# A transformer block with a mixture of 16384 experts on one core: the matrix of gates added into DRAM entry by entry in place of one-hot matrix products, and deeper rings of loaded data

## The chip, the cores and the metric

The kernel runs on one core of one Trainium2 chip. The metric is the time of one execution in microseconds (us) on the device, given as the median of several runs. A core has five engines that work side by side: PE multiplies matrices, DVE does vector operations, ACT does activations and copies, POOL does general work and issues indirect DMAs, SP issues DMAs. They wait for each other through semaphores. Sixteen DMA engines carry what SP, ACT and POOL issue.

## What is computed

The program is a block with retention and sparse attention, a convolutional feed-forward part, then a second block with a gated recurrence and, last, the part that the change is in: PEER, a layer of 16384 experts of which each of the 512 tokens uses 8 x 16.

```python
def peer(h, w_query, sub_keys, expert_u, expert_v):
    ...
        q = (xb @ w_query).reshape(T, PEER_HEADS, 2, PEER_HALF)
        s = jnp.einsum('thpk,hpnk->thpn', q, sub_keys).astype(jnp.float32)
        top_s, top_i = lax.top_k(s, PEER_TOPK)
        cand_s = top_s[:, :, 0, :, None] + top_s[:, :, 1, None, :]
        cand_i = top_i[:, :, 0, :, None] * PEER_NKEYS + top_i[:, :, 1, None, :]
        best_s, best_pos = lax.top_k(cand_s.reshape(T, PEER_HEADS, PEER_TOPK * PEER_TOPK), PEER_TOPK)
        idx = jnp.take_along_axis(cand_i.reshape(T, PEER_HEADS, PEER_TOPK * PEER_TOPK), best_pos, axis=-1)
        gate = jax.nn.softmax(best_s, axis=-1)
        ...
        act = jax.nn.gelu(jnp.einsum('td,thkd->thk', xb, u).astype(jnp.float32), approximate=False)
        return jnp.einsum('thk,thkd->td', (gate * act).astype(xb.dtype), v)
```

## The kernel before

All matrices stream through a ring of four chunks of 512 KB. For each chunk SP loads RAW, ACT rounds it to WH (`split_high`, a "high"), DVE computes the rest WL (`split_low`, a "low"), and PE multiplies by three products (`mm3`, lines 272 to 274). A high waits until PE has used the chunk four before it. The order of the work on each engine is written out by hand, as numbers of chunks.

The last two stages belong to the experts. In the **u stage** (144 chunks `p`, of which 16 are the query matrix) PE computes the product of all 512 tokens with the 128 keys of every chunk, ACT applies gelu (`gelu`, L1101), and SP keeps the result in DRAM (`acts`). At the same time DVE finds for each tile `t` of 128 tokens the 16 best of each list (`pairs`), subtracts the largest (`shifted`), and turns places into the numbers n1 and n2 of the expert (`summed`, with a comparison prepared on POOL by `places_apart`, L795). `listed` ends it with the softmax weight.

For three of the four tiles (ND = 3) the gates must lie in DRAM as a matrix of experts by tokens. PE turns the three lists (L2184), DVE writes for 8 tokens at a time one-hot rows of n1 and of n2 times weight (`onehot_rows`, L1707 and L1710, from a difference that POOL makes at L807), PE multiplies them (`gates_of`, L2172, 48 groups n), ACT moves the products to a staging area (`store_gates`, L1123) and stores it six times (L1126). The fourth tile goes another way: POOL picks its rows of `peer_v` (L814, `pick_row`) and single activations (L822, `pick_acts`), and DVE sums them (L1739, `sum_row`).

In the **v stage** (128 chunks `v`) ACT loads gates and acts for four chunks at a time (`load_group`, L1129 and L1130, a ring of two groups), DVE multiplies them (`weights`, L1719), ACT takes the high part (L1135), DVE the low part WGL (L1723), and PE multiplies both with the chunk of `peer_v`. The first two groups are loaded by ACT in chunk p = QU - 6 = 138 of the u stage:

```python
                if p == QU - 6:
                    for r in range(2):
                        act.wait_ge(sem(f"gates_written{r}"), 16 * NU // 2)
                    ...
                    for j in range(2):
                        load_group(j)
```

`low_of_next(n)` does the next n lows; `lows[0]` counts them. L267 is the low, L261 the high.

Of the kernel before, what the change touches and what calls it, by code (L numbers as in the profile page):

```python
# [21 lines left out]
P = 128  # L22
# [23 lines left out]
NU = DW // 64  # L46
NG8 = 8 * NU
PICKS = PH * TOPK
SLOTS = 6
# [30 lines left out]
LOWS_LISTED = (47, 59, 71, 77)  # L80
LOWS_SHIFTED = (35, 47, 59, 71)


def before_gates(n):
    return 80 + 3 * n // 4

def constants():  # L90
# [27 lines left out]
    cols["token"] = (GT_TILE * P + i[:, None]).astype(f)  # L118
# [7 lines left out]
    for n, m in enumerate((64, 32, 16, 8, 4, 2, 1)):  # L126
# [7 lines left out]
              ("causal", P), ("cmp_ok", NT * 32), ("cmp_no", NT * 32), ("iota", P), ("four", 4), ("token", 1)]  # L134
# [12 lines left out]
def build(nc, d):  # L147
# [3 lines left out]
    with ExitStack() as ctx:  # L151
# [485 lines left out]
        LST = [A[:, 21504:21888], A[:, 21888:22272], XF[:, 0:384]]  # L637
        LST = [x.rearrange("p (l t) -> p l t", l=3) for x in LST]
        APART = XF[:, 2048:4096].rearrange("p (r i n) -> p r i n", r=2, i=8)
        zg, zs8 = misc(8), misc(8)  # L640

        HALF = 64
        STG = A[:, 0:16384].rearrange("p (r i t) -> p r i t", r=2, i=P)
        OHA = A[:, 16384:18432].rearrange("p (r n) -> p r n", r=16)
        OHB = A[:, 18432:20480].rearrange("p (r n) -> p r n", r=16)

        ACTED = [GATE[:, 0, 0:512], GATE[:, 0, 512:1024], ROW[:, 0:512], ROW[:, 512:1024]]
        G4 = A[:, 0:8 * DW].rearrange("p (r u i t) -> p r u i t", r=2, u=NU, i=4)
        AC = A[:, 8 * DW:16 * DW].rearrange("p (r i t) -> p r i t", r=2, i=4)
        WGHr = over("A", "WGH", 16 * DW, 4 * DW, F32R).rearrange("p (r t) -> p r t", r=4)  # L650
        WGLr = over("A", "WGL", 20 * DW, 4 * DW, F32R).rearrange("p (r t) -> p r t", r=4)
        WGH = WGHr.bitcast(F32)
        WF = A[:, 24 * DW:26 * DW].rearrange("p (r t) -> p r t", r=2)


        ROWS = A[:, 26 * DW:26 * DW + SLOTS * D].rearrange("p (r n) -> p r n", r=SLOTS)
        assert 26 * DW + SLOTS * D <= 16384
# [12 lines left out]
        acts_kept = nc.dram_tensor("acts", (P, P, S), F32, kind="Internal").ap()  # L670
        act_list = acts_kept.rearrange("e p (t o) -> (e p t) o", o=1)
# [75 lines left out]
        def _(pool):  # L747
# [35 lines left out]
            pool.dma_start(ROW[:, :], dr["nf_post"].partition_broadcast(P)).then_inc(sem("row_landed"), 16)  # L783
            pool.wait_ge(sem("rows_weighted"), 2 * NT)
# [5 lines left out]
            def places_apart(t, i):  # L790

                wait(pool, "eq_summed", 4 * t + i)
                p3 = PAB.rearrange("p s u -> p (s u)")[:, i * 64:i * 64 + 64].rearrange("p (h k) -> p h k", k=TOPK).unsqueeze(3)
                it = con("iota")[:, 0:TOPK].unsqueeze(1).unsqueeze(1)
                nc.gpsimd.tensor_tensor(EQ, p3.to_broadcast([P, PH // 2, TOPK, TOPK]),  # L795
                                        it.to_broadcast([P, PH // 2, TOPK, TOPK]), ALU.subtract).then_inc(sem("eq_ready"), 1)
# [5 lines left out]
            pool.wait_ge(sem("list_stored"), ND)  # L802
            pool.wait_ge(sem("picks_listed"), 1)
            for n in range(NG8):
                wait(pool, "onehot_ready", n - 1)
                nums = LST[n // 16][:, 1, 8 * (n % 16):8 * (n % 16) + 8].unsqueeze(2).to_broadcast([P, 8, P])
                nc.gpsimd.tensor_tensor(APART[:, n % 2], con("iota").unsqueeze(1).to_broadcast([P, 8, P]), nums,  # L807
                                        ALU.subtract).then_inc(sem("rows_apart"), 1)

# [16 lines left out]
            for r in range(2):  # L826
                pool.wait_ge(sem(f"gates_written{r}"), 16 * NU // 2)
# [16 lines left out]
        def _(act):  # L844
# [268 lines left out]
            gm = dr["gate_matrices"]  # L1113

            def store_gates(n):
                u = n // 8
                if n % 8 == 0:
                    wait(act, f"gates_written{u % 2}", 16 * (u // 2))
                for b in (2 * n, 2 * n + 1):
                    act.wait_ge(sem("gm_ready"), b + 1)  # L1120
                    at = 4 * (b % 16)
                    dst = STG[:, u % 2].rearrange("p i t -> p t i")[:, at:at + 4, :]
                    nc.scalar.activation(dst, PS[:, b % 4, :].rearrange("p (t n) -> p t n", t=4), ACT.Copy)                        .then_inc(sem("gm_stored"), 1)  # L1123
                if n % 8 == 7:
                    act.wait_ge(sem("gm_stored"), 16 * (u + 1))
                    act.dma_start(gm[u], STG[:, u % 2]).then_inc(sem(f"gates_written{u % 2}"), 16)  # L1126
# [10 lines left out]
            for p in range(24, QU):  # L1137
                high_of_next()
                gelu(u_of(p))
                for t in range(NT):  # L1140
                    if p == LOWS_SHIFTED[t] - 3:
                        act.wait_ge(sem("best_shifted"), t + 1)
                        nc.scalar.activation(BV[:, t % 2], BV[:, t % 2], ACT.Exp).then_inc(sem("best_exp"), 1)
                    if t < ND and p == LOWS_LISTED[t] - 2:
                        act.wait_ge(sem("list_turned"), t + 1)
                        nc.scalar.activation(LST[t], PS[:, 4, 0:3 * P].rearrange("p (l t) -> p l t", l=3), ACT.Copy)                            .then_inc(sem("list_stored"), 1)
                for n in range(NG8):
                    if before_gates(n) == p + 1:
                        store_gates(n)
                if p == QU - 6:  # L1150
                    for r in range(2):
                        act.wait_ge(sem(f"gates_written{r}"), 16 * NU // 2)
                    for r in range(4):
                        act.wait_ge(sem(f"acts_kept{r}"), 16 * 2)
                    for j in range(2):
# [33 lines left out]
        def _(dve):  # L1189
# [289 lines left out]
            for m in range(28):  # L1479
# [12 lines left out]
                if m == 6:  # L1492
                    dve.wait_ge(sem("hg_exps"), 1)
                    link(nc.vector.tensor_tensor_scan(flat(BB), flat(SC8), flat(HF), 0.0, ALU.mult, ALU.add))
# [146 lines left out]
            def summed(t, i):  # L1641

                dve.wait_ge(sem("eq_ready"), 4 * t + i + 1)
                for h in range(PH // 2):
                    num = TFf[:, i * 64 + 16 * h:i * 64 + 16 * h + TOPK].unsqueeze(1).to_broadcast([P, TOPK, TOPK])
                    last = nc.vector.scalar_tensor_tensor(EQ[:, h], EQ[:, h], 0.0, num, ALU.is_equal, ALU.mult)
                last.then_inc(sem("eq_numbers"), 1)
                dve.wait_ge(sem("eq_numbers"), 4 * t + i + 1)
                nc.vector.tensor_reduce(N12[:, t % 2].rearrange("p s u -> p (s u)")[:, i * 64:i * 64 + 64],
                                        EQ.rearrange("p h k a -> p (h k) a"), AX, ALU.add).then_inc(sem("eq_summed"), 1)  # L1650

            def listed(t):
                assert lows[0] == LOWS_LISTED[t]
                dve.wait_ge(sem("best_exp"), t + 1)
                dve.wait_ge(sem("eq_summed"), 4 * t + 4)
                link(nc.vector.tensor_reduce(zg, BV[:, t % 2], AX, ALU.add))
                link(nc.vector.reciprocal(zg, zg))
                if t < ND:
                    nc.vector.tensor_tensor(BV[:, t % 2], BV[:, t % 2], zg.unsqueeze(2).to_broadcast([P, PH, TOPK]),
                                            ALU.mult).then_inc(sem("list_ready"), 1)  # L1660
                else:
                    n1, n2 = N12[:, t % 2, 0], N12[:, t % 2, 1]
                    nc.vector.tensor_tensor(GW.rearrange("p (h k) -> p h k", h=PH), BV[:, t % 2],
                                            zg.unsqueeze(2).to_broadcast([P, PH, TOPK]), ALU.mult)
                    link(nc.vector.scalar_tensor_tensor(EXPERT, n2, float(P), n1, ALU.mult, ALU.add))
# [17 lines left out]
            for s_ in range(NT + 1):  # L1683
# [9 lines left out]
                if s_ < NT:  # L1693
                    until(last)
# [579 lines left out]
```

## Time and profile before

| | |
|---|---|
| median of 3 runs | 2643.19 us (2641.51 to 2643.9) |
| the profiled execution | 2637.98 us |
| its span in the trace | 2636.1 us |
| PE busy | 2519.1 us, 96% |
| DVE busy | 1579.1 us, 60% |
| ACT busy | 1027.7 us, 39% |
| POOL busy | 502.8 us, 19% |
| DMA traffic | 434.03 MB, mean 165 GB/s |

Busy times are sums over the instructions of an engine in one profiled execution. An engine that is idle costs nothing unless another waits for it. The time of an execution is that of the span and some 2 us around it.

### The profile page before, as it was taken

Reading aid. Unit: us, or ns where it says so; the run is one execution under the profiler, and the core shown is the slowest. Engines: PE = TensorE matmul, PEld = TensorE weight load, DVE = VectorE, ACT = ScalarE, POOL = GpSimd, SP = SyncE. Lnnn points to the kernel's source line nnn. Section 1 sums busy time; section 2 is a strip of 40 time slices with the busy share of each in tenths; the row PEclk is TensorE's granted clock in tenths of the full one; section 3 lists DMA queues with packets and bytes.
Section 4 is the critical chain, followed back from the end, with each engine's and each line's share of the span. In section 5 each row is a group of like instructions: output and inputs, shape, how many; then the busy total and the mean of one; then the engine's idle time right before and its main releaser. Section 6 shows DMA issues by size and latency. Waiting matters only on the chain.

```text
span 2636.1 us, 31762 instructions
## 1 busy us (share of the span) xinstructions
PE 2519.1 (96%) x11982; PEld 2081.6 (79%) x11982; DVE 1579.1 (60%) x2604; ACT 1027.7 (39%) x1452; POOL 502.8 (19%) x363
## 2 busy tenths in 40 slices
PE   7999998999999999899999999999999999899995
PEld 6876676888888788778888888888888778777784
DVE  4365665555543577467767755556322777777777
ACT  4353443433332644543333334555422333333332
POOL 0030000000000000000011123333100755566651
PEclk9997999999999999999999999999999999999998
DMA  6223343233322222133344443546645899889994
GB/s 207 82 67 97 94 137 99 85 98 99 97 96 96 80 80 72 57 117 104 122 146 144 144 144 139 205 160 229 236 146 190 308 329 334 310 320 320 316 336 145
DMA packets 162696, 434.03 MB, mean 165 GB/s; under 512 B 17072, under 2 KB 59072, under 8 KB 161280
## 3 DMA queue, kind: packets, MB, share of 16 engines
q1 hardware_dynamic: 94896, 276.96, 31.6%
q10 hardware_dynamic: 43424, 77.60, 8.4%
q0 software_dynamic: 24240, 77.63, 7.9%
q8 instruction: 89, 1.46, 0.2%
q14 instruction: 47, 0.39, 0.0%
HBM read 369.21 MB, written 62.91 MB: 164 GB/s over the span
## 4 chain that ended last, share of the span: by engine, by line
PE 71%; DVE 11%; DMA 8%; issue 4%; ACT 4%; POOL 1%; ACTq 0%; DVEq 0%; SPq 0%; POOLq 0%
PE PS L272 20%; PE PS L274 20%; PE PS L273 20%; DVE WL L267 4%; DMA A<-acts 4%; DMA A<-gate_matrices 3%; DVE PS L1739 3%; PE PS L2172 3%; DVE A L1719 2%; ACT WGH L1135 1%; PE PS L1935 1%; PE PS L2072 1%; PE PS L2019 1%; PE PS L2006 1%; POOL A L822 1%
## 5 line engine op out<-in xcount | busy, mean ns | idle before, releaser
L267 DVE TENSOR_TENSOR WL<-RAW,WH 128x1024 fp32r<-128x1024 f32 x462 | 587.1, 1272 | 557.9 <-ACT WH L261 520.6
L272 PE MATMUL PS<-HH,WH 128*128 128x512 f32 x1696 | 667.4, 394 | 8.8 <-DVE HL L433 7.1
L273 PE MATMUL PS<-HL,WH 128*128 128x512 f32 x1696 | 660.8, 390 | 0.0
L274 PE MATMUL PS<-HH,WL 128*128 128x512 f32 x1696 | 660.8, 390 | 0.0
L261 ACT ACTIVATE WH<-RAW 128x1024 fp32r<-128x1024 f32 x462 | 485.2, 1051 | 247.5 <-PE PS L274 209.6
L272 PEld LDWEIGHTS PS<-HH,WH 128*128 128x128 f32 x1696 | 318.8, 188 | 79.2 <-DVE HL L433 10.3
L274 PEld LDWEIGHTS PS<-HH,WL 128*128 128x128 f32 x1696 | 318.6, 188 | 66.6
L273 PEld LDWEIGHTS PS<-HL,WH 128*128 128x128 f32 x1696 | 318.9, 188 | 63.4
L272 PE MATMUL PS<-WH,WGH 128*128 128x512 f32 x768 | 307.2, 400 | 39.4 <-DVE WGL L1723 38.6
L273 PE MATMUL PS<-WL,WGH 128*128 128x512 f32 x768 | 304.8, 397 | 0.0
L274 PE MATMUL PS<-WH,WGL 128*128 128x512 f32 x768 | 304.4, 396 | 0.0
L814 POOL DMA_INDIRECT A<-in_peer_v,V_AT x128 | 187.9, 1468 | 225.7 <-DVE PS L1739 176.9
L272 PEld LDWEIGHTS PS<-WH,WGH 128*128 128x128 f32 x768 | 148.1, 193 | 75.4 <-issue 43.3
L1135 ACT ACTIVATE WGH<-A 128x384 fp32r<-128x384 f32 x128 | 67.2, 525 | 335.6 <-DVE A L1719 333.9
L273 PEld LDWEIGHTS PS<-WL,WGH 128*128 128x128 f32 x768 | 148.4, 193 | 30.9
L274 PEld LDWEIGHTS PS<-WH,WGL 128*128 128x128 f32 x768 | 147.8, 192 | 31.5
L1739 DVE SCALAR_TENSOR_TENSOR PS<-A,PS 128x1024 f32<-128x1024 f32 x127 | 163.0, 1283 | 2.1 <-DVE A L1732 0.6
L822 POOL DMA_INDIRECT A<-acts,A_AT x128 | 147.2, 1150 | 48.9 <-issue 38.7
L272 PE MATMUL PS<-WH,HH 128*128 128x512 f32 (+1 forms) x352 | 137.5, 391 | 12.5 <-DVE A L1554 5.5
L273 PE MATMUL PS<-WL,HH 128*128 128x512 f32 (+1 forms) x352 | 136.0, 386 | 0.0
L274 PE MATMUL PS<-WH,HL 128*128 128x512 f32 (+1 forms) x352 | 136.0, 386 | 0.0
L1101 ACT ACTIVATE ROW<-PS 128x512 f32<-128x512 f32 x64 | 38.3, 598 | 235.7 <-PE PS L274 235.7
(338 smaller groups left out, 3077.8 us busy)
## 6 DMA issues: line engine op xcount, KB each, us to landing
RAW<-in_peer_u SPq DMA_DIRECT2D x128, 512.0 KB, 3.5
RAW<-in_peer_v SPq DMA_DIRECT2D x128, 512.0 KB, 7.0
RAW<-in_w_ada SPq DMA_DIRECT2D x48, 512.0 KB, 3.7
gate_matrices<-A ACTq DMA_DIRECT2D x6, 4096.0 KB, 12.6
A<-gate_matrices ACTq DMA_DIRECT2D x32, 768.0 KB, 7.9
A<-acts ACTq DMA_DIRECT2D x32, 768.0 KB, 13.0
RAW<-in_ffn_up SPq DMA_DIRECT2D x44, 512.0 KB, 3.4
acts<-GATE SPq DMA_DIRECT2D x64, 256.0 KB, 2.3
```

Of the source, the lines that this page charges most:

```text
L261: nc.scalar.activation(WHr[:, slot(c), 0:w], RAW[:, slot(c), 0:w], ACT.Copy).then_inc(sem("high_done"), 1)
L267: nc.vector.tensor_tensor(WLr[:, slot(c), 0:w], RAW[:, slot(c), 0:w], WH[:, slot(c), 0:w], ALU.subtract).then_inc(sem("low_done"), 1)
L272: nc.tensor.matmul(out, L[0], R[0], start=first, stop=False)
L273: nc.tensor.matmul(out, L[0], R[1], start=False, stop=False)
L274: return nc.tensor.matmul(out, L[1], R[0], start=False, stop=last)
L814: pool.indirect_dma_start(out=ROWS[:, u % SLOTS, :], out_offset=None, in_=dr["peer_v"], in_offset=bass.IndirectOffsetOnAxis(ap=V_AT[:, u:u ...
L822: pool.indirect_dma_start(out=AG[:, u:u + 1], out_offset=None, in_=act_list, in_offset=bass.IndirectOffsetOnAxis(ap=A_AT[:, u:u + 1], axis ...
L1101: nc.scalar.activation(ACTED[k % 4], PS[:, 5 + k % 3, :], ACT.Gelu).then_inc(sem("gelu_done"), 1)
L1135: nc.scalar.activation(WGHr[:, v % 4, :], WF[:, v % 2, :], ACT.Copy).then_inc(sem("w_high"), 1)
L1719: nc.vector.tensor_tensor(WF[:, v % 2, :].rearrange("p (u t) -> p u t", u=NU), AC[:, j % 2, v % 4, :].rearrange("p (u t) -> p u t", u=NU), ...
L1739: ins = nc.vector.scalar_tensor_tensor(ACC, row, PW[:, u:u + 1], ACC, ALU.mult, ALU.add)
L2172: last = nc.tensor.matmul(PS[:, b % 4, j * P:(j + 1) * P], OHA[:, r, :], OHB[:, r, :], start=True, stop=True)
```

## The change

The gates of the first three tiles are now written into a DRAM tensor `gates` of 128 x 128 x 384 numbers. POOL fills it with zeros by 16 DMAs during the stage "up" of the feed-forward part. When DVE has listed a tile, POOL issues 128 indirect DMAs for it; each takes one pick of all 128 tokens, and adds 128 single weights to 128 single places in DRAM. Before each new head (16 picks) it waits until all earlier DMAs of the tile have landed. The one-hot rows, their products, the evictions, the staging and the stores go. DVE does the comparison in `summed` itself, and the tiles are now listed one after the other. The groups of gates and acts are loaded in a ring of three (GROUPS) in place of two, asked for at v % 4 == 1 in place of 2, and the row picks have seven slots in place of six.

```diff
-SLOTS = 6
+SLOTS = 7
+GROUPS = 3
...
-LOWS_LISTED = (47, 59, 71, 77)
-LOWS_SHIFTED = (35, 47, 59, 71)
...
+LOWS_SHIFTED = (35, 48, 61, 74)
...
+            nc.gpsimd.memset(ZERO, 0.0).then_inc(sem("zero_set"), 1)
+            pool.wait_ge(sem("zero_set"), 1)
+            for n in range(16):
+                pool.wait_ge(sem("chunk_used"), FIRST["up"] + 2 * n + 1)
+                pool.dma_start(gates_kept.rearrange("e p t -> p e t")[:, 8 * n:8 * n + 8, :],
+                               ZERO.unsqueeze(1).to_broadcast([P, 8, DW])).then_inc(sem("gates_zeroed"), 16)
...
-            for t in range(NT):
-                pool.wait_ge(sem("places_ready"), t + 1)
-                for i in range(4):
-                    places_apart(t, i)
...
+            pool.wait_ge(sem("gates_zeroed"), 16 * 16)
+            for t in range(ND):
+                pool.wait_ge(sem("gates_listed"), t + 1)
+                for u in range(PICKS):
+                    if u >= TOPK and u % TOPK == 0:
+                        pool.wait_ge(sem(f"gates_placed{t}"), 16 * u)
+                    pool.indirect_dma_start(out=gate_list, out_offset=bass.IndirectOffsetOnAxis(ap=PLACE[:, t, u:u + 1], axis=0),
+                                            in_=SHARES[:, t, u:u + 1], in_offset=None, compute_op=ALU.add)\
+                        .then_inc(sem(f"gates_placed{t}"), 16)
...
-                act.dma_start(G4[:, j % 2], gm.rearrange("u p i t -> p u i t")[:, 0:NU, 4 * j:4 * j + 4, :])                    .then_inc(sem(f"gates_landed{j % 2}"), 16)
-                act.dma_start(AC[:, j % 2], acts_kept.rearrange("e p t -> p e t")[:, 4 * j:4 * j + 4, 0:DW])                    .then_inc(sem(f"acts_landed{j % 2}"), 16)
+                es = slice(4 * j, 4 * j + 4)
+                act.dma_start(G4[:, j % GROUPS], gates_kept.rearrange("e p t -> p e t")[:, es, :])\
+                    .then_inc(sem(f"gates_landed{j % GROUPS}"), 16)
+                act.dma_start(AC[:, j % GROUPS], acts_kept.rearrange("e p t -> p e t")[:, es, 0:DW])\
+                    .then_inc(sem(f"acts_landed{j % GROUPS}"), 16)
...
                 if p == QU - 6:
-                    for r in range(2):
-                        act.wait_ge(sem(f"gates_written{r}"), 16 * NU // 2)
+                    for t in range(ND):
+                        act.wait_ge(sem(f"gates_placed{t}"), 16 * PICKS)
...
-                if v % 4 == 2 and 2 <= v // 4 + 2 < P // 4:
-                    j = v // 4 + 2
+                if v % 4 == 1 and v // 4 + GROUPS < P // 4:
+                    j = v // 4 + GROUPS
...
-                    act.wait_ge(sem("w_done"), 4 * (j - 1))
+                    act.wait_ge(sem("w_done"), 4 * (j - GROUPS + 1))
```

On POOL this is the piece between the load of the subkeys and the picks of the fourth tile, in the kernel before (names: `in_peer_v` is the table of rows, `acts` the kept activations, A the large scratch area):

```order
L788 DMA A<-in_subk 128x2048
L795 TENSOR_TENSOR A<-X,CON 128x1024 x16
L807 TENSOR_TENSOR X<-CON,A 128x1024 x32
L807 TENSOR_TENSOR X<-CON,X 128x1024 x16
L814 DMA A<-in_peer_v,V_AT 128x1024 x6
L831 DMA HH_scratch<-x 128x4096
L822 DMA A<-acts,A_AT 128x1 x8
```

and this the same piece in the changed kernel:

```order
L786 DMA A<-in_subk 128x2048
L794 DMA gates<-A,PLACE 6291456x1 x384
L801 DMA A<-in_peer_v,V_AT 128x1024 x7
L817 DMA HH_scratch<-x 128x4096
L809 DMA A<-acts,A_AT 128x1 x8
```

The 64 tensor operations are gone, and 384 indirect DMAs stand ahead of the row picks.

On ACT, in the second half of the u stage, the kernel before alternates a high, a gelu and evictions of the one-hot products, with a store after every eighth group:

```order
L261 ACTIVATE WH<-RAW 128x1024
L1101 ACTIVATE GATE<-PS 128x512
L1123 ACTIVATE A<-PS 128x4x128 x2
L1126 DMA gate_matrices<-A 128x8192
L261 ACTIVATE WH<-RAW 128x1024
L1101 ACTIVATE GATE<-PS 128x512
L1123 ACTIVATE A<-PS 128x4x128 x4
```

and the changed kernel has at p = QU - 6 this, where the loads stand behind the wait for all adds:

```order
L253 ACTIVATE WH<-RAW 128x1024
L1087 ACTIVATE ROW<-PS 128x512
L1101 DMA A<-gates 128x4x384
L1103 DMA A<-acts 128x4x384
L1101 DMA A<-gates 128x4x384
L1103 DMA A<-acts 128x4x384
L1101 DMA A<-gates 128x4x384
L1103 DMA A<-acts 128x4x384
L253 ACTIVATE WH<-RAW 128x1024
```

The evictions and stores are gone, and six loads stand where four stood, ahead of the next high.

On DVE, the end of the first tile (after `shifted`) reads in the changed kernel:

```order
L259 TENSOR_TENSOR WL<-RAW,WH 128x1024
L1614 TENSOR_TENSOR A<-X,CON 128x1024
L1618 TENSOR_TENSOR A<-A,X 128x256 x4
L1620 TENSOR_REDUCE X<-A 128x64
L259 TENSOR_TENSOR WL<-RAW,WH 128x1024
L1626 TENSOR_REDUCE MISC<-X 128x8
L1627 RECIPROCAL MISC<-MISC 128x8
L1629 TENSOR_TENSOR A<-X,MISC 128x128
L1631 SCALAR_TENSOR_TENSOR A<-X 128x128
L1634 SCALAR_TENSOR_TENSOR PLACE<-A,CON 128x128
```

The first four rows stand there four times; L1614 is the comparison that POOL prepared before, and L1634 writes the places that POOL waits for.

## Rows read from the trace of the kernel before

**Rows 1.** The page: busy us, share of the span and instructions of each engine.
```profile
PE 2519.1 (96%) x11982; PEld 2081.6 (79%) x11982; DVE 1579.1 (60%) x2604; ACT 1027.7 (39%) x1452; POOL 502.8 (19%) x363
```

**Rows 2.** Windows: length; busy (count) of PE, PEld, DVE, ACT, POOL; clock, DMA share, GB/s.
```profile
1335.00:1570.00 235.00, 235.00 (x1043) 194.53 (x1042) 162.50 (x377) 79.18 (x101) 39.37 (x16) 1.00 0.45 145
...
1878.00:2007.00 129.00, 129.00 (x571) 106.80 (x570) 29.44 (x24) 36.62 (x47) 6.36 (x6) 1.00 0.55 200
...
2035.00:2612.00 577.00, 538.05 (x2290) 440.49 (x2291) 432.44 (x522) 193.30 (x254) 329.75 (x252) 0.96 0.88 311
```

**Rows 3.** Waits of PE, 2040 to 2612 us: total, times, longest.
```profile
PE PS L272 <- DVE WGL L1723: 38.6, 10, 6.9
```

**Rows 4.** Waits of DVE, 2062 to 2612 us: total, times, longest.
```profile
DVE WGL L1723 <- ACT WGH L1135: 71.5, 121, 0.6
DVE A L1719 <- issue: 46.1, 8, 8.8
DVE A L1719 <- DMA A<-acts: 8.1, 1, 8.1
```

**Rows 5.** The chain that ended last, 1850 to 2150 us: start, us, what.
```profile
2117.17 0.57 DVE A L1719
2117.93 16.00 DMA A<-gate_matrices
2133.93 7.46 issue
```

**Rows 6.** Landing times of L1130 (acts), then of L822.
```profile
DMA to landing us min/median/max: 6.6/13.0/23.8
DMA to landing us min/median/max: 2.3/5.0/8.1
```

**Rows 7.** Timeline of DVE, two starts of L1723, twelve chunks apart.
```profile
2142.54 0.56 DVE L1723 TENSOR_TENSOR WGL<-A,WGH 128x384 fp32r<-128x384 f32 x1 [0.59 <-ACT WGH L1135]
2190.66 0.56 DVE L1723 TENSOR_TENSOR WGL<-A,WGH 128x384 fp32r<-128x384 f32 x1 [0.59 <-ACT WGH L1135]
```

**Rows 8.** Timeline of ACT: gelus of two chunks, five apart, and a high between them.
```profile
2007.41 0.60 ACT L1101 ACTIVATE ROW<-PS 128x512 f32<-128x512 f32 x1 [3.89 <-PE PS L274]
...
2018.79 1.05 ACT L261 ACTIVATE WH<-RAW 128x1024 fp32r<-128x1024 f32 x1
...
2034.61 0.60 ACT L1101 ACTIVATE ROW<-PS 128x512 f32<-128x512 f32 x1 [3.48 <-PE PS L274]
```

**Rows 9.** The chain on PE, 1595 to 1640 us; then the transposes as a group.
```profile
1600.18 3.57 PE PS L2172 x32
...
1623.68 3.57 PE PS L2172 x32
L2184 PE MATMUL PS<-CON,X 128*128 128x128 f32 x9 | 1.5, 271 | 0.0
```

**Rows 10.** Timeline of DVE: the first low after `shifted(0)`, and products and sum of `summed`.
```profile
1339.58 1.23 DVE L267 TENSOR_TENSOR WL<-RAW,WH 128x1024 fp32r<-128x1024 f32 x1 [2.97 <-ACT WH L261]
...
1347.79 1.43 DVE L1646 SCALAR_TENSOR_TENSOR A<-A,X 128x256 f32<-128x256 f32 x4
1349.25 1.22 DVE L1649 TENSOR_REDUCE X<-A 128x64 f32<-128x1024 f32 x1
```

**Rows 11.** Group of DVE: count, busy us, mean ns, idle before.
```profile
L1707 DVE TENSOR_TENSOR A<-CON,A 128x1024 f32<-128x1024 f32 x32 | 39.8, 1243 | 34.3 <-PE PS L2172 34.3
```

**Rows 12.** Window of the up stage.
```profile
540.00:790.00 250.00, 250.00 (x1104) 207.01 (x1104) 131.26 (x155) 87.29 (x116) 0.00 (x0) 1.00 0.30 97
```

**Rows 13.** Timeline of POOL: first and last of six row picks ahead of the v stage.
```profile
1891.41 1.01 POOL L814 DMA_INDIRECT A<-in_peer_v,V_AT  x1 [32.71 <-DMA gate_matrices<-A]
...
1898.35 0.94 POOL L814 DMA_INDIRECT A<-in_peer_v,V_AT  x1 [0.30 <-issue]
```

**Rows 14.** Groups of POOL: count, busy us, mean ns, idle before.
```profile
L814 POOL DMA_INDIRECT A<-in_peer_v,V_AT x128 | 187.9, 1468 | 225.7 <-DVE PS L1739 176.9 <-DMA gate_matrices<-A 32.7 <-issue 16.1
L822 POOL DMA_INDIRECT A<-acts,A_AT x128 | 147.2, 1150 | 48.9 <-issue 38.7 <-DMA acts<-ROW 10.2
```

More of the change, by code:

```diff
@@ L670, in build @@
         acts_kept = nc.dram_tensor("acts", (P, P, S), F32, kind="Internal").ap()
+        gates_kept = nc.dram_tensor("gates", (P, P, DW), F32, kind="Internal").ap()
+        gate_list = gates_kept.rearrange("e p (t o) -> (e p t) o", o=1)
         act_list = acts_kept.rearrange("e p (t o) -> (e p t) o", o=1)
@@ L1143, in _ @@
                         nc.scalar.activation(BV[:, t % 2], BV[:, t % 2], ACT.Exp).then_inc(sem("best_exp"), 1)
[L1144 to L1149, printed above, removed]
                 if p == QU - 6:
-                    for r in range(2):
-                        act.wait_ge(sem(f"gates_written{r}"), 16 * NU // 2)
+                    for t in range(ND):
+                        act.wait_ge(sem(f"gates_placed{t}"), 16 * PICKS)
                     for r in range(4):
-                        act.wait_ge(sem(f"acts_kept{r}"), 16 * 2)
-                    for j in range(2):
+                        act.wait_ge(sem(f"acts_kept{r}"), 16 * GROUPS)
+                    for j in range(GROUPS):
                         load_group(j)
@@ L1644, in summed @@
                 for h in range(PH // 2):
                     num = TFf[:, i * 64 + 16 * h:i * 64 + 16 * h + TOPK].unsqueeze(1).to_broadcast([P, TOPK, TOPK])
[L1646 to L1650, printed above, removed]
+                    last = nc.vector.tensor_tensor(EQ[:, h], EQ[:, h], num, ALU.mult)
@@ L1652, in listed @@
+                link(last)
+                link(nc.vector.tensor_reduce(N12[:, t % 2].rearrange("p s u -> p (s u)")[:, i * 64:i * 64 + 64],
+                                             EQ.rearrange("p h k a -> p (h k) a"), AX, ALU.add))
             def listed(t):
-                assert lows[0] == LOWS_LISTED[t]
                 dve.wait_ge(sem("best_exp"), t + 1)
-                dve.wait_ge(sem("eq_summed"), 4 * t + 4)
+                n1, n2 = N12[:, t % 2, 0], N12[:, t % 2, 1]
                 link(nc.vector.tensor_reduce(zg, BV[:, t % 2], AX, ALU.add))
@@ L1680, in shifted @@
                 nc.vector.tensor_copy(TF, TI[:, t].rearrange("p (h s) k -> p s h k", s=2))
[L1681 to L1684 removed]
+                link(nc.vector.tensor_copy(PAB, PABu))
+            for t in range(NT):
                 for i in range(4):
                     low_of_next()
[L1687 to L1711 removed]
+                    last = pairs(t, i)
+                    low_of_next()
+                until(last)
+                shifted(t)
+                for i in range(4):
+                    low_of_next()
+                    summed(t, i)
+                low_of_next()
+                listed(t)
             def weights(v):
@@ L1740, in sum_row @@
                 ins.then_inc(sem("rows_summed"), 1)
-            dve.wait_ge(sem("list_stored"), ND)
-            for n in range(NG8):
-                low_of_next(before_gates(n) + 2 - lows[0])
-                onehot_rows(n)
             low_of_next(QU + 1 - lows[0])
@@ L2164, in _ @@
             score(15)
-            def gates_of(n):
-                pe.wait_ge(sem("onehot_ready"), n + 1)
-                for b in (2 * n, 2 * n + 1):
-                    wait(pe, "gm_stored", b - 3)
-                    for j in range(4):
-                        r = 8 * (n % 2) + 4 * (b % 2) + j
-                        last = nc.tensor.matmul(PS[:, b % 4, j * P:(j + 1) * P], OHA[:, r, :], OHB[:, r, :],
-                                                start=True, stop=True)
-                    last.then_inc(sem("gm_ready"), 1)
             pe.wait_ge(sem("scores_stored"), 16)
@@ L2178, in _ @@
                 acts(u_of(p))
-                for t in range(NT):
-                    if t < ND and p == LOWS_LISTED[t] - 2:
-                        pe.wait_ge(sem("list_ready"), t + 1)
-                        wait(pe, "list_stored", t)
-                        for l, src in enumerate((N12[:, t % 2, 0], N12[:, t % 2, 1], BV[:, t % 2].rearrange("p h k -> p (h k)"))):
-                            last = nc.tensor.transpose(PS[:, 4, l * P:(l + 1) * P], src, ident)
-                        last.then_inc(sem("list_turned"), 1)
-                for n in range(NG8):
-                    if before_gates(n) == p + 1:
-                        gates_of(n)
             pe.wait_ge(sem("gelu_done"), P)
```

116 lines of the change are left out of this document (33 added, 83 removed).

## The prediction

> **What bounds the kernel now.** I read the page first: PE is busy for 96% of the span of 2636.1 us [rows 1]. An engine that is busy so long is the bound nearly everywhere, so the next view is a table of windows over the last stages. It shows three regimes [rows 2]. From 1335 to 2007 us PE is busy in every microsecond, at granted clock 1.00, while DVE falls from 69% to 23%. From 2035 to 2612 us (the v stage) PE has 538 of 577 us, the clock falls to 0.96 and the DMA engines are busy for 0.88 of the time. The waits of PE confirm it for the v stage: 38.6 us, ten times, for WGL, a product of DVE [rows 3]. So in the u stage only what is taken from PE counts; in the v stage, what makes DVE late.
>
> What makes DVE late is in its own waits [rows 4]. 71.5 us go to the short turn through ACT in every chunk. The others are long: 8.1 us for the load of acts, and 46.1 us in eight waits in front of the same instruction (L1719, the product of gates and acts), each at the first chunk of a group of four. "issue" means that the view names no releaser. The chain does: at 2117.93 a gate load takes 16.00 us, and 7.46 us more pass before L1719 starts [rows 5]; the acts load that is issued behind it can take 23.8 us [rows 6], so that one came last. Undisturbed, DVE goes from L1723 to L1723 in (2190.66 - 2142.54) / 12 = 4.01 us [rows 7]. PE needs 18 matmuls a chunk; the u stage has 24 in (2034.61 - 2007.41) / 5 = 5.44 us [rows 8], so 4.08 us. The two are equal, and a stall of DVE is never made good: 54.2 us of stalls become 38.6 us of waiting PE, and the lower clock takes most of the rest.
>
> **What is taken from PE.** The 48 groups of one-hot products go. In the chain four of them lie in one period, 1600.18 to 1623.68, which also holds three chunks: (23.50 - 3 x 5.44) / 4 = 1.80 us each, 86.2 us together [rows 8, 9]. The nine transposes of the lists take 1.5 us [rows 9]. Nothing else fills PE there, so 87.7 us come off the path. The 96 evictions on ACT and the six stores of 4 MB go with them, and were hidden.
>
> **What moves to DVE.** DVE loses 96 one-hot operations of about 1.24 us, some 120 us [rows 11], and gets 16 comparisons of 1024 elements that stood on POOL, at 1.24 us. One step of `summed` is then a low (1.23), a comparison (1.24), four products (1.43 together), a sum (1.22) and some 0.3 us of links: 5.4 us, against 5.44 us per chunk [rows 8, 10, 11]. It just fits, and the lows run a chunk ahead, so I cost it at nothing. Without that cover a tenth of a microsecond in 16 steps would be 2 us.
>
> **Zeroing.** 16 DMAs of 1.5 MB go out during the up stage, 25 MB, as much as the gate stores that go. There the DMA engines are busy for 0.30 and PE waits for nothing [rows 12]. At the 97 GB/s of that row plus 25 MB in 174 us (32 chunks) it becomes some 240 GB/s, below the 311 GB/s of the v stage [rows 2]. Nothing; if a raw chunk came late, a few us.
>
> **The adds on POOL.** This is the term that decides. 384 indirect DMAs of 128 single elements, each read, added and written in DRAM, with a wait for landing before every group of 16 from the second on, 21 in all. No row shows an accumulating DMA. The nearest is L822, an indirect read of 128 single elements. The shortest row pick has 0.94 of work and 0.30 of issue in front, 1.25 us together; the six row picks issued while DVE was nearly idle stand (1898.35 - 1891.41) / 5 = 1.39 us apart [rows 13]. L822's mean is 1.15, with the gap 1.45; the row picks, 1.47, make 1.77 [rows 14]. Landing takes 2.3 to 8.1 us, median 5.0, in a stage with 0.88 of DMA time [rows 6, 2]; in the u stage the share is 0.45 to 0.55, and I take 3.5. So 384 x 1.40 = 538 us, and 21 waits of 3.5 - 1.4, 44 us.
>
> They start when the first tile is listed. After `shifted(0)` come five lows at the pace of 5.44 from 1339.58, so 1361.3 + 1.2 + 1.6 of small operations = 1364 us [rows 10, 8]. End: 1364 + 538 + 44 + 2 (the last landing) = 1948 us.
>
> Who waits: ACT, at p = QU - 6, ahead of the first loads. Before, this place was right behind the gelu of 2007.41 [rows 8]; without the 87.7 us it is 1920. Queued behind the wait are the next highs and gelus; behind POOL's own waits stand the next adds, then seven row picks, the reload of X3 and the first picks of acts, which in any case wait for the last gelu. ACT also issues six loads there in place of four, 1.0 us more. PE starts chunk p = 142 three chunks after 2007.4, at 2023.7, and needs high (1.05) and low (1.23) before; so ACT may be held until 2021, 14 us. The first group's landing and its products have about as much. The adds are thus late by 1948 - 1934 = 14, with the restart 15 us. Lower bound of this term: 384 x 1.25 + 21 x (2.3 - 1.25) ends at 1364 + 480 + 22 = 1866, late by nothing. Upper bound from rows: 384 x 1.77 + 21 x (8.1 - 1.8) + 6 ends at 2182, late by 248. The middle is nearest to L822 itself.
>
> The Trainium skill has two rules that bear on it. "DMA: Bandwidth & Descriptors", section "Anatomy of one DMA — SWDGE (gpsimd) path", gives such a DMA some 2.0 us of fixed cost, mostly the write receipt, longest when the target is HBM; by that the 21 waits would be 13 us (an estimate) in place of 44. The adds would then end at 1917, before ACT asks, and the time would be rival 1's; the trace agrees at its lower end, 2.3 us. "SBUF — State Buffer", section "SBUF: two separate sides", says that POOL cannot write descriptors while DVE holds the shared port; L814 takes 0.94 us at its shortest and 1.47 in the mean [rows 13, 14], which could be it, but no run here shows the cause; if DVE's small operations held it up as often as in the v stage, the time would go toward rival 2.
>
> **The deeper rings.** A group was asked for 15.5 us before DVE wanted it (2117.93 to about 2133.4, four cycles after L1719 at 2117.17), and landed after up to 23.8. With three groups in flight and the request one slot earlier it gets five cycles more, 15.5 + 20 = 35.6 us, above the longest landing. All 54.2 us of stalls may go. Without them DVE ends its products 121 x 4.01 after 2061, at 2546, and PE the last chunks at about 2559, against 2615 before: 56 us. The demand rises with the pace, so I leave 6 for a stall that stays, and take 50. The bounds are 0 and 56. The gate rows become runs of 1.5 KB in place of 1 KB, which lightens the DMA a little. The seventh row slot answers no wait of the trace: nothing.
>
> **Sum.** The profiled execution took 2638.0 us, 5.2 less than the median. 2638.0 - 87.7 - 50 + 15 = 2515; against the median, 2520.
>
> **Rivals.** (1) Adds well hidden, at the lower bound: no 15, so 2505. The idle POOL before 1891 and the light DVE after 1590 speak for it. (2) The adds cost more than a read, since each has two sources: slower than before. At 1.77 us with landings of 5.0 the end is 1364 + 680 + 67 + 3 = 2114, late by 180, and the time 2643 - 138 + 180 = 2685. It decides from 1934 + 138 = 2072 us on, that is from 1.84 us per add with its share of the waits; I have 1.52. Against it: POOL's work for single elements, 1.15, lies between the shortest and the mean for rows of 4 KB, 0.94 and 1.47, so its price does not go by what is moved. (3) The group stalls stay, because the DMA engines are full (0.88 busy already, and the same bytes would have to move in less time): 2520 + 50 = 2570. (4) Both in part, adds 40 to 130 us late: 2545 to 2635.
>
> **Chances.** Forecast (late 0 to 40 us, rings work), with rival 1 inside it: 0.57. Rival 3: 0.12. Rival 4: 0.08. Rival 2: 0.22, of which some 0.15 lie above 2660. A little, 0.01, for no change. This kernel tells 0.2%, 5 us, from nothing. Faster 0.76, within it 0.02, slower 0.22. The range goes from 2498, where both gains are whole, to 2660.
>
> **What would show it.** PE without the 128x128 products between the u chunks, last gelu near 1947 plus the lateness; spacing of the adds 1.4 us and 21 gaps of about 2; ACT's wait ahead of the first gate load near 1948, PE idle then about 15 us; in the v stage no wait of L1719 for a landing, clock above 0.96. The prediction is wrong if the adds stand 1.8 us or more apart, or if POOL's wait per head is nearer to 10 us.

## The result, and the profile after

The changed kernel takes 2742.18 us (median of 4 runs, 2738.9 to 2744.11) against 2643.55 us for the kernel before: slower, ratio 1.0373 with a 95% interval of 1.0355 to 1.0391. The profile is of an execution with a span of 2742.0 us.

These are the span and the busy times from the page of the changed kernel, and in the last line the shares of the chain that ended last:

```profile
span 2742.0 us, 30322 instructions
PE 2417.5 (88%) x11205; PEld 1985.4 (72%) x11205; DVE 1464.8 (53%) x2530; ACT 937.3 (34%) x1353; POOL 988.8 (36%) x700
...
PE 62%; POOL 21%; issue 6%; DVE 4%; DMA 4%; ACT 2%; ACTq 1%; DVEq 0%; SPq 0%; POOLq 0%
```

PE went from 96% [rows 1] to 88% of a longer span, and POOL, which had 1% of the chain before, has 21%. The windows of the last stages (length; busy time and count of PE, PEld, DVE, ACT, POOL; clock, DMA share, GB/s) show where:

```profile
1900.00:1925.00 25.00, 25.00 (x112) 20.70 (x111) 4.88 (x4) 5.24 (x7) 21.04 (x14) 1.00 0.63 136
1925.00:2100.00 175.00, 11.43 (x51) 9.14 (x49) 0.00 (x0) 0.00 (x0) 137.68 (x90) 0.55 0.21 0
...
2195.00:2720.00 525.00, 517.30 (x2274) 425.92 (x2273) 431.68 (x520) 194.60 (x250) 321.74 (x250) 1.00 0.93 335
```

Until 1925 us PE is full. In the next 175 us it works off 11.4 us that were ready and then stops; DVE and ACT do nothing, only POOL works, and the DMA engines move next to nothing (0 GB/s). From 2195 us on the v stage runs better than before [rows 2]: PE has 517 of 525 us, at clock 1.00 in place of 0.96. The waits of PE from 1800 us on have one long entry, the first of these two (total, times, longest):

```profile
PE PS L264 <- DVE WL L259: 238.9, 1, 238.9
PE PS L264 <- DVE WGL L1675: 4.8, 4, 1.5
```

The entry that answers to [rows 3] is the second: 4.8 us where there were 38.6. The first is new. DVE waited there for ACT, and the timeline of ACT shows for what:

```profile
1920.15 0.60 ACT L1087 ACTIVATE ROW<-PS 128x512 f32<-128x512 f32 x1 [3.89 <-PE PS L266]
2158.18 0.40 ACTq L1101 DMA_DIRECT2D A<-gates  x1
...
2161.50 11.24 ACTq L1103 DMA_DIRECT2D A<-acts  x1
2172.84 1.06 ACT L253 ACTIVATE WH<-RAW 128x1024 fp32r<-128x1024 f32 x1 [252.09 <-issue]
```

ACT reaches chunk QU - 6 at 1920.15, which was 2007.41 in [rows 8]: 87.3 us earlier. It then waits until 2158.18 for the last add to land, and the sixth load holds it for 11.24 us more. The groups of POOL (count, busy us, mean ns, idle before) give the price of an add:

```profile
L794 POOL DMA_INDIRECT gates<-A,PLACE x384 | 617.0, 1607 | 399.7 <-DVE PLACE L1634 225.7 <-issue 129.5 <-DMA gates<-A,PLACE 44.6
```

An add takes 1.607 us of POOL in the mean, where the read of single elements took 1.150 [rows 14]. The timeline of POOL while DVE and ACT stand shows it undisturbed, with the landing wait of one head at the end:

```profile
1930.92 1.55 POOL L794 DMA_INDIRECT gates<-A,PLACE  x1 [0.30 <-issue]
1932.77 1.55 POOL L794 DMA_INDIRECT gates<-A,PLACE  x1 [0.30 <-issue]
1935.99 1.55 POOL L794 DMA_INDIRECT gates<-A,PLACE  x1 [1.67 <-DMA gates<-A,PLACE]
```

Undisturbed, the adds start 1.85 us apart. From the first at 1365.50 to the last at 2155.03 they take 789.5 us, 2.06 us each with all waits. The third row is the first add of a head, issued when all earlier adds of its tile had landed. It takes 1.55 us too, so a queue that is full of adds is not what makes an add long.

The v stage itself, from the first to the last product with WGH (first and last start of PE's instructions in the row), is 531.6 us long; it was 2035.3 to 2614.6, 579.3 us:

```profile
L264 PE MATMUL PS<-WH,WGH x768: 388/389/500, 2189.2 to 2720.8; 128*128 128x512 f32 x192
```

So the balance of the two traces is 2636.1 - 87.3 (gates off PE) + 238.9 (PE waits) - 47.7 (v stage) = 2740.0, against 2742.0.

### The profile page after: what moved, and what is told of

Same layout as the page of the kernel before. It is cut to its first block, busy times and chain, and to the rows that moved or that the text cites. A ratio compares the mean times of both kernels' runs of the same rounds, so it can differ in the third digit from the quotient of the medians.

```text
span 2742.0 us, 30322 instructions
## 1 busy us (share of the span) xinstructions
PE 2417.5 (88%) x11205; PEld 1985.4 (72%) x11205; DVE 1464.8 (53%) x2530; ACT 937.3 (34%) x1353; POOL 988.8 (36%) x700
## 4 chain that ended last, share of the span: by engine, by line
PE 62%; POOL 21%; issue 6%; DVE 4%; DMA 4%; ACT 2%; ACTq 1%; DVEq 0%; SPq 0%; POOLq 0%
POOL gates L794 21%; PE PS L264 18%; PE PS L266 18%; PE PS L265 18%; DMA gates<-A,PLACE 3%; PE PS L1883 1%; PE PS L2020 1%; PE PS L1967 1%; DVE WL L259 1%; PE PS L1954 1%; PE PS L408 1%; ACT WH L253 1%; PE PS L2098 1%; PE PS L414 0%; DMA RAW<-in_w_in 0%
## 5 line engine op out<-in xcount | busy, mean ns | idle before, releaser
L259 DVE TENSOR_TENSOR WL<-RAW,WH 128x1024 fp32r<-128x1024 f32 x462 | 564.3, 1222 | 886.5 <-ACT WH L253 878.5
L264 PE MATMUL PS<-HH,WH 128*128 128x512 f32 x1696 | 665.1, 392 | 247.6 <-DVE WL L259 238.9
L794 POOL DMA_INDIRECT gates<-A,PLACE x384 | 617.0, 1607 | 399.7 <-DVE PLACE L1634 225.7
L264 PE MATMUL PS<-WH,WGH 128*128 128x512 f32 x768 | 299.4, 390 | 7.8 <-DVE WGL L1675 4.8
L266 PE MATMUL PS<-WH,WGL 128*128 128x512 f32 x768 | 298.9, 389 | 0.6 <-issue 0.5
L265 PE MATMUL PS<-WL,WGH 128*128 128x512 f32 x768 | 298.8, 389 | 0.0
L801 POOL DMA_INDIRECT A<-in_peer_v,V_AT x128 | 175.3, 1370 | 151.9 <-DVE PS L1691 131.2
L809 POOL DMA_INDIRECT A<-acts,A_AT x128 | 152.5, 1191 | 47.7 <-issue 38.7
L266 PEld LDWEIGHTS PS<-WH,WGL 128*128 128x128 f32 x768 | 144.1, 188 | 30.8 <-issue 0.7
```

Of the source, the lines that this page charges most:

```text
L259: nc.vector.tensor_tensor(WLr[:, slot(c), 0:w], RAW[:, slot(c), 0:w], WH[:, slot(c), 0:w], ALU.subtract).then_inc(sem("low_done"), 1)
L264: nc.tensor.matmul(out, L[0], R[0], start=first, stop=False)
L265: nc.tensor.matmul(out, L[0], R[1], start=False, stop=False)
L266: return nc.tensor.matmul(out, L[1], R[0], start=False, stop=last)
L794: pool.indirect_dma_start(out=gate_list, out_offset=bass.IndirectOffsetOnAxis(ap=PLACE[:, t, u:u + 1], axis=0), in_=SHARES[:, t, u:u + 1], ...
L801: pool.indirect_dma_start(out=ROWS[:, u % SLOTS, :], out_offset=None, in_=dr["peer_v"], in_offset=bass.IndirectOffsetOnAxis(ap=V_AT[:, u:u ...
```

## The experiments

The ratios below stand against runs of the kernel before on the same chip, 2643.97 us for the first three and 2641.1 us for the rest. The latter is 2.5 us below the 2643.55 of the changed kernel's own comparison, so where a few us matter, differences to the changed kernel are told by the ratios as well. The first three experiments leave out or lose some weights; the others compute the whole layer.

**Writes in place of adds**

```diff
                     pool.indirect_dma_start(out=gate_list, out_offset=bass.IndirectOffsetOnAxis(ap=PLACE[:, t, u:u + 1], axis=0),
-                                            in_=SHARES[:, t, u:u + 1], in_offset=None, compute_op=ALU.add)\
+                                            in_=SHARES[:, t, u:u + 1], in_offset=None)\
```

> The changed kernel, but the 384 indirect DMAs write their weights in place of adding them (where two heads pick the same expert for a token, one weight is lost; nothing else is left out). Theory A: an accumulating DMA costs POOL 1.55 us to issue where one that only moves costs 0.95, and that price sets the end of the adds. Then the spacing falls from 1.85 to 1.25 us, the last of them lands near 1365 + 384 x 1.25 + 21 x 2 = 1890 us, before ACT asks at 1920, PE does not stop, and the time is 2742 - 241 = about 2502 us. Theory B: the writes of 4 bytes into DRAM hold the queue back, whatever is computed. Then the spacing stays near 1.85 and the time near 2742 us.

Measured: 2518.02 us (2515.31 to 2519.35), ratio 0.9519 (0.9497 to 0.9541). POOL's group in the trace of this kernel:

```profile
L794 POOL DMA_INDIRECT gates<-A,PLACE x384 | 404.9, 1054 | 386.4 <-DVE PLACE L1634 225.7 <-issue 120.6 <-DMA gates<-A,PLACE 40.1
```

A row of the timeline:

```profile
1879.84 0.97 POOL L794 DMA_INDIRECT gates<-A,PLACE  x1 [0.30 <-issue]
```

The price falls to 0.97 us undisturbed and 1.05 in the mean, and 224 us of the time go with it. Theory B, a queue held back by the small writes, falls. The time is 16 us above theory A's 2502, since a write with the gap in front of it takes (1932.28 - 1367.65 - 40.1) / 384 = 1.37 us in the mean and not 1.25. The rest is a small copy of the changed kernel's trouble: the last write lands at 1934.5, ACT loads 12.3 us late, and PE waits once. The timeline of ACT:

```profile
1922.30 0.60 ACT L1087 ACTIVATE ROW<-PS 128x512 f32<-128x512 f32 x1 [3.90 <-PE PS L266]
1934.56 0.40 ACTq L1101 DMA_DIRECT2D A<-gates  x1
...
1938.26 10.54 ACTq L1103 DMA_DIRECT2D A<-acts  x1
```

PE's wait:

```profile
PE PS L264 <- DVE WL L259: 12.8, 1, 12.8
```

ACT's next high starts at 1948.90, so ACT is held for 26.6 us, 12.3 by the late writes and 14.3 by the six loads. PE waits for 12.8 of them, so 13.8 us are tolerated, as the prediction has it (14). The 10.54 us of the last load are most of those 12.8.

**Half of the adds**

```diff
-                for u in range(PICKS):
+                for u in range(PICKS // 2):
...
-                        act.wait_ge(sem(f"gates_placed{t}"), 16 * PICKS)
+                        act.wait_ge(sem(f"gates_placed{t}"), 16 * PICKS // 2)
```

> The changed kernel with only the first four of the eight heads added (192 DMAs in place of 384; the weights of the other heads are left out of the first three tiles). Theory A: the price of the adds is paid only because they end late; 192 x 2.06 us end near 1765 us, all hidden, and the time is about 2742 - 241 = 2501 us. Theory B: the late end is only part, and the restart of ACT costs by itself, since its six loads hold it for 14.7 us (one of them took 11.2 us to issue) also when the adds are early; then some us to 10 us more, 2505 to 2512 us. Theory C: the adds slow the chunks of PE down through DRAM or the DMA engines; then clearly more than 2512 us.

Measured: 2499.79 us (2499.09 to 2505.7), ratio 0.9455 (0.943 to 0.948). Theory A. The adds here are as dear as in the changed kernel (1.648 us in the mean), but they are done before ACT asks, and PE's waits from 1300 us on are 4.6 us in all. So the adds cost nothing but their late end, and the new listing is hidden. The six loads hold ACT for 6.4 us, the last of them for 3.23, and PE does not wait for them.

**A price list**

```diff
+                    ps = slice(0, 64) if t == 1 and u < 64 or t == 2 and u >= 64 else slice(0, P)
-                    pool.indirect_dma_start(out=gate_list, out_offset=bass.IndirectOffsetOnAxis(ap=PLACE[:, t, u:u + 1], axis=0),
-                                            in_=SHARES[:, t, u:u + 1], in_offset=None, compute_op=ALU.add)\
+                    pool.indirect_dma_start(out=gate_list, out_offset=bass.IndirectOffsetOnAxis(ap=PLACE[ps, t, u:u + 1], axis=0),
+                                            in_=SHARES[ps, t, u:u + 1], in_offset=None, **({} if t == 0 or t == 2 and u >= 64 else dict(compute_op=ALU.add)))\
```

> The changed kernel with four kinds of indirect DMA for the price list (weights are lost or left out in the first three tiles): the first tile only writes, with 128 partitions; in the second the first 64 DMAs add with 64 partitions and the rest with 128; in the third the first 64 add with 128 and the last 64 write with 64. Theory A, POOL's work on descriptors sets the price: write of 128 is 0.95 us, add of 128 1.55, add of 64 lies between 0.9 and 1.3, write of 64 below 0.95. Theory B, the far end holds POOL back: write and add of 128 cost the same 1.55. The rows of POOL tell it apart; the time should lie between those of the changed kernel and of the one that only writes, near 2610 us.

Measured: 2603.5 us (one run). The timeline of POOL, one row of each kind, in this order: write of 128, add of 64, add of 128, write of 64.

```profile
1490.92 0.97 POOL L795 DMA_INDIRECT gates<-A,PLACE  x1 [0.31 <-issue]
1599.64 1.41 POOL L795 DMA_INDIRECT gates<-A,PLACE  x1 [0.30 <-issue]
1723.23 1.54 POOL L795 DMA_INDIRECT gates<-A,PLACE  x1 [0.30 <-issue]
1967.81 0.91 POOL L795 DMA_INDIRECT gates<-A,PLACE  x1 [0.30 <-issue]
```

Two things follow. It is the adding that is dear, in the same kernel and stage: 1.54 against 0.97 us. And the add of 64 elements, 1.41, lies above the 0.9 to 1.3 that theory A expected: the extra price is 0.50 us at 64 elements and 0.57 at 128, so most of it is there once per DMA and does not come with the elements. Halving the elements saves 0.13 us. Theory B, the same price for a write and an add, falls. What POOL does in the 0.57 us is not told by these runs.

**The ring of three in the kernel before.** A first form, with a semaphore for each load, could not be built and gave no result; in this one a group's two loads share a semaphore.

```diff
+GROUPS = 3
...
-                if v % 4 == 2 and 2 <= v // 4 + 2 < P // 4:
-                    j = v // 4 + 2
+                if v % 4 == 1 and v // 4 + GROUPS < P // 4:
+                    j = v // 4 + GROUPS
...
-                    dve.wait_ge(sem(f"gates_landed{j % 2}"), 16 * (j // 2 + 1))
-                    dve.wait_ge(sem(f"acts_landed{j % 2}"), 16 * (j // 2 + 1))
+                    dve.wait_ge(sem(f"group_landed{j % GROUPS}"), 32 * (j // GROUPS + 1))
```

> The kernel before with only the ring of gates and acts made three groups deep and the request one slot earlier (the two loads of a group share a semaphore). Theory A: the depth of the ring alone takes the 47.5 us off the v stage that the changed kernel shows, so 2643 - 47 = about 2596 us, with no wait of DVE in front of the product of gates and acts. Theory B: it needed the longer runs of the new layout (1.5 KB in place of 1 KB) or the seventh row slot as well; then less than half of it, 2620 us or more.

Measured: 2588.73 us (2587.17 to 2589.93), ratio 0.9808 (0.979 to 0.9826), so 52 us less than the kernel before. Waits of DVE from 2062 to 2560 us, all there are:

```profile
DVE WGL L1723 <- ACT WGH L1136: 71.6, 121, 0.6
DVE WL L268 <- ACT WH L262: 0.3, 1, 0.3
```

The 54.2 us in front of the product of gates and acts [rows 4] are gone, all of them, and the short turn through ACT is as it was. Theory A: three groups, asked for one slot earlier, do it alone, with the old layout and six row slots. Which part the earlier request has was not tried.

**The heads of three tiles take turns**

```diff
-            for t in range(ND):
-                pool.wait_ge(sem("gates_listed"), t + 1)
-                for u in range(PICKS):
-                    if u >= TOPK and u % TOPK == 0:
-                        pool.wait_ge(sem(f"gates_placed{t}"), 16 * u)
+            heads = sorted([(h + 2 * t, t, h) for t in range(ND) for h in range(PH)])
+            for _, t, h in heads:
+                if h == 0:
+                    pool.wait_ge(sem("gates_listed"), t + 1)
+                else:
+                    pool.wait_ge(sem(f"gates_placed{t}"), 16 * TOPK * h)
+                for u in range(TOPK * h, TOPK * h + TOPK):
```

> The changed kernel with the same adds in another order: the heads of the three tiles take turns, so that between two heads of one tile mostly a head of another tile is issued, and its landing covers the wait. Theory A: the 21 waits between heads cost only their 44.6 us; 17 of them go, 17 x 2.1 = 36 us, so 2742 - 36 = about 2706 us, still slower than before. Theory B: the waits also let the queue run empty and full again and cost more than their length; then 2690 us or less.

Measured: 2688.14 us (2687.39 to 2692.51), ratio 1.0189 (1.0168 to 1.0209). By the ratios that is (1.0373 - 1.0189) x 2643 = 49 us less than the changed kernel, more than the 36 of theory A. The median meets theory B's 2690; with the 2.5 us between the two comparisons added it would be 2690.7, so the time alone does not decide. The waits of POOL:

```profile
POOL gates L796 <- issue: 115.5, 379, 0.3
POOL gates L796 <- DMA gates<-A,PLACE: 9.4, 4, 3.6
```

The landing waits went from 44.6 to 9.4 us, 35.2 as expected. The "issue" time went from 129.5 to 115.5 us though there are more entries: its longest is 0.3 us now, and was 3.6. In the changed kernel nine gaps between adds are 1.87 to 3.56 us long and not 0.30, at the 61st, 114th and 121st add of each tile, and with nearly the same lengths in the next experiment's trace too. Together they make 129.5 - 115.5 + 17 x 0.30 = 19 us. What they are stays open. Theory B's emptied queue would show behind each landing wait; three of the nine (the 114th) stand one add behind one, the other six and the other landing waits do not fit. With the writes in place of the adds only those at the 114th are there.

**The third group later**

```diff
-                    for j in range(GROUPS):
+                    for j in range(2):
                         load_group(j)
+                if p == QU - 3:
+                    load_group(2)
```

> The changed kernel with only two of the three first groups loaded in chunk QU - 6 and the third three chunks later. Theory A: the restart after the late adds costs 11 us because ACT issues six loads at once and the last of them holds it for 11.2 us; with four loads PE restarts about 9 us earlier, 2733 us. Theory B: the restart is set by the landing of the first group and by the lower clock of PE; then no change, 2742 us.

Measured: 2732.14 us (2731.45 to 2737.14), ratio 1.0355 (1.0334 to 1.0376), so between 5 us (by the ratios) and 10 us less. The size of theory A's 9 us is not told by the times, whose intervals overlap, but the trace shows its mechanism: PE's waits up to the v stage fall from 239.6 to 232.7 us (6.0 of them are a new wait for ACT), and the first product with WGH starts at 2181.9 in place of 2189.2. ACT's next high comes at 2160.83 in place of 2172.84:

```profile
2158.20 0.40 ACTq L1101 DMA_DIRECT2D A<-gates  x1
...
2160.83 1.06 ACT L253 ACTIVATE WH<-RAW 128x1024 fp32r<-128x1024 f32 x1 [239.88 <-issue]
...
2161.68 15.29 ACTq L1103 DMA_DIRECT2D A<-acts  x1
```

The last row shows that the sixth load is not cheaper in its new place: it takes 15.29 us, now behind the first highs and not ahead of them.

What fills these microseconds shows in windows over the long load, here of the changed kernel and then of the one with half of the adds (length; busy and count of PE, PEld, DVE, ACT, POOL; clock, DMA share, GB/s):

```profile
2161.50:2172.80 11.30, 0.00 (x0) 0.00 (x0) 0.00 (x0) 0.00 (x0) 2.98 (x4) 0.50 1.03 396
1922.60:1929.40 6.80, 6.80 (x32) 5.63 (x31) 0.00 (x0) 0.43 (x1) 0.00 (x0) 1.00 0.84 267
```

In the changed kernel the DMA engines are full. The seven row picks that stood on POOL behind the last add are issued at 2156.89 to 2164.46, at the same time as the six loads; with half of the adds they had gone out from 1769.31 on. In all five traces in which the picks meet the loads the sixth load takes 9.75 to 15.29 us. In the three in which they had gone out before (half of the adds, the ring in the kernel before, and the mixed kernel below) it takes 2.02 to 3.23. No run moves the picks alone, so the cause is likely but not shown.

**Adds for two tiles, products for the third.** At 2.06 us each POOL can place some 280 adds between 1365 and about 1950 us, when ACT asks if a third of the one-hot products stay, and the ring is worth its 50 us in any case.

```diff
+ADDED_TILES = 2
+NG8 = 16
...
-            for t in range(ND):
+            for t in range(ADDED_TILES):
                 pool.wait_ge(sem("gates_listed"), t + 1)
...
+                if n % 8 == 7:
+                    act.wait_ge(sem("gm_stored"), 16 * (u + 1) + 1)
+                    at = P * ADDED_TILES + 64 * u
+                    act.dma_start(gates_kept.rearrange("e p t -> p e t")[:, :, at:at + 64], STG[:, u])\
+                        .then_inc(sem("gates_written"), 16)
...
+            for n in range(NG8):
+                low_of_next(before_gates(n) + 1 - lows[0])
+                onehot_rows(n)
```

(`onehot_rows`, `gates_of` and `store_gates` are those of the kernel before, for 16 groups from chunk 92 on, one every two chunks.)

> Adds for the first two tiles only, one-hot products for the third (16 of the 48 groups, both comparisons on DVE, stored into the same tensor), ring of three groups, six row slots; it computes the whole reference. Theory A: the adds fill POOL for 2.06 us each, 256 of them end near 1365 + 527 = 1892 us, before ACT asks (about 1950); PE pays 16 x 1.8 + 0.5 = 29 us for the third tile. 2643.5 - 87.3 + 29.3 - 47.5 = about 2538 us, faster than both kernels. Theory B: the work that DVE gets (48 operations of 1.24 us) and the stores of 4 MB in runs of 256 bytes make the u stage late; then 2550 us or more.

Measured: 2531.5 us (2529.43 to 2534.77), ratio 0.9592 (0.9573 to 0.9611): 4.1% faster than the kernel before, and it computes the whole layer. PE's waits from 1300 to 2500 us, all there are:

```profile
PE PS L270 <- DVE WGL L1711: 5.0, 3, 2.2
PE PS L270 <- ACT ROW L1098: 0.7, 1, 0.7
```

The timeline of POOL at the end of the adds, and of ACT at chunk QU - 6:

```profile
1919.66 1.55 POOL L804 DMA_INDIRECT gates<-A,PLACE  x1 [0.30 <-issue]
1921.51 1.01 POOL L811 DMA_INDIRECT A<-in_peer_v,V_AT  x1 [0.30 <-issue]
...
1950.90 0.60 ACT L1098 ACTIVATE ROW<-PS 128x512 f32<-128x512 f32 x1 [3.89 <-PE PS L272]
```

The adds end some 30 us later than the 1892 that I expected: a mean add took 1.689 us in place of 1.607 (21 us for 256), and the 14 waits were longer, 37.9 us. That is still ahead of ACT, which comes to its wait 30.8 us later than in the changed kernel (29 forecast for the third tile's products). PE does not wait in the u stage. Theory A; the result is 6 us under its number, and 2 us by the ratio (0.9592 x 2643.5 = 2535.7).

## Why the prediction was wrong

**What bounds the kernel** held for the kernel before: what was taken from PE in the u stage and the stalls taken from DVE in the v stage both came back as time.

**Taken from PE**: 87.7 us forecast; ACT's place at QU - 6 came 87.3 us earlier. Right.

**Moved to DVE, and the zeroing**, costed at nothing: right. PE's waits from 500 to 800 us, around the zeroing, are 0.9 us in both kernels. With half of the adds PE waits 4.6 us in all from 1300 us on. The first add starts at 1365.5 (1364 forecast), so the listing came when it should.

**The adds on POOL**: this term failed, and it decided. Its start was right, and so were its waits, 44.6 us for 21 where I had 44. The price of one add was not: "so 384 x 1.40 = 538 us". It was (789.5 - 44.6) / 384 = 1.94 us, 745 us together. Undisturbed the add is 1.55 + 0.30, in place of the 0.94 + 0.30 of an indirect DMA that only moves. I took the nearest row, a read of single elements, as if adding were free on POOL. With the writes in place of adds the same program shows how near the rest was: 1.27 us apart undisturbed and 1.37 in the mean, so that the 1.40 is nearly the price of a write; the last landing at 1934.5 (I had 1948), PE 12.8 us idle (I had 15), and 2518.0 us (I had 2520). That the idle time agrees is luck: the writes ended where I had the limit, 1934, so nearly all of the 12.8 us come from the six loads, to which I had given 1 us of my 15. The adding alone is 2742.2 - 2518.0 = 224 us, the whole distance between forecast and result. The bounds from rows held: the upper one ended at 2182, the adds at 2158. That an add could be dearer than a read was named in rival 2. No run tests the reason that it gave, two sources. Its point of decision, 1.84 us per add with waits, was passed by 2.06. Rival 2's 2685 us was 57 too low, since it had 1.77 and not 1.94, and no price for the restart. The middle that I took had no reason beyond nearness, and the range cut the upper bound off.

**The restart**: forecast as 1 us over a tolerance of 14. The tolerance was right: ACT's next high came 252.7 us after it reached QU - 6, and PE waited for 238.9 of them, so 13.8 us cost nothing; the writes give 13.8 us too. The restart was dearer, 14.7 us for the six loads, of which the sixth has 11.24. In the sum I had left out the four loads of before (2007.63 to 2011.12 in the trace before) and the row picks that go out at the same time, when the DMA engines are full. Loading the third group later gave 5 to 10 us back. So the adds landed 2158.2 - 1934 = 224 us late, and 15 us of restart, 239 together.

**The deeper rings**: 50 us forecast, 47.7 in the v stage of the changed kernel, 52 in the kernel before with the ring alone. Right, and by the mechanism: no wait of DVE in front of the product of gates and acts is left in either kernel. Rival 3, that full DMA engines would keep the stalls, fell: the share rose to 0.93 and DVE found each group landed.

**The two rules of the Trainium skill.** The landing waits took 44.6 us. In the chain an add lands 2.96 to 3.08 us after its issue began when the other engines stand, and 3.01 to 4.80 us before 1925; 1.55 of that is issue. By the Trainium skill's fixed cost (DMA: Bandwidth & Descriptors, section "Anatomy of one DMA — SWDGE (gpsimd) path"), about 2.0 us, the waits would have been 13 us (an estimate), so the trace does not agree with the estimate for adds. A write in their place lands after 2.13 us at the shortest, which is near it. The 1.55 us of an add stand while DVE does nothing; over the stages in which DVE works the mean is higher by some 0.1 (1.64 us up to 1925 us, and 1.69 in the mixed kernel). By the Trainium skill's rule on the shared port (SBUF — State Buffer, section "SBUF: two separate sides") POOL cannot write descriptors while DVE holds that port. It could explain the 0.1, which was not tried, but not the failure.

## What to carry to other kernels

Where work is moved to an engine that is off the path, count it against the moment at which someone waits for its last piece: here 2.06 us times 384 against the 555 us from the first add to ACT's wait. A price 0.54 us too low, 384 times, made 207 us. An operation that no row shows is not priced by its nearest relative when the sum turns on it; take the share of it that fits under every bound, as the mixed kernel does, which pays some 30 us on PE and lost nothing when its adds ended 30 us later than thought. And two changes in one should be judged apart: the ring of three was worth 2%, and the loss of the adds hid it.

## What the runs showed of the hardware that I had not expected

- An indirect DMA issued by POOL with one element for each of 128 partitions costs it 0.97 us when it writes and 1.54 when it adds; with 64 partitions it costs 0.91 and 1.41. These are the undisturbed values, and in all of them 0.30 us of issue stand in front.
- The sixth load in a row on ACT's queue took 11.24 us to issue (9.75 to 15.29 in four other traces) where seven row picks of 512 KB were issued beside it; in the changed kernel the DMA engines were full then, at a share of 1.03. It took 3.23 us with half of the adds and 2.02 in the mixed kernel, where the picks had gone before and the share was 0.84 and 0.79. The cause is not separated.
- After 239 us without work PE restarts with ten matmuls of 0.77 to 0.61 us in place of 0.39. The granted clock is 0.51 in the idle stretch from 1937 to 2175 us and 0.53 from 2175 to 2180 us, the lower of its two levels (1.2 GHz), and 1.00 (2.4 GHz) from 2180 to 2195 us.
- Nine gaps of 1.9 to 3.6 us between adds, at the same places of each tile, vanish when the heads take turns. Their cause is open.
